# The first twelve weight units of a two-block transformer kernel: one low half on GpSimd, two filler matmuls gone, requests and norm rows in another order

## The reference, cut to what matters

```
mem_n = rmsnorm(mem, mem_norm)
mem_kv = mem_n @ w_mem_kv[i]                  # mk, mv: keys and values of the memory
h = rmsnorm(x, norm_mix[i])
proj = h @ a_w_in[i]
u, b_gate, c_gate, q_mem = jnp.split(proj, ...)
y_tok = _short_conv(u, b_gate, c_gate, a_conv_w[i])
y_mem = _mem_attention(q_mem, mk, mv)
x = x + jnp.concatenate([y_tok, y_mem], axis=-1) @ w_out
```

## Time and profile before

| | |
|---|---|
| median of 3 runs | 930.21 us (928.26 to 930.96) |
| profiled execution, its own time | 925.97 us |
| its span, first to last instruction | 924.2 us |
| PE busy | 913.8 us (99%) |
| DVE busy | 680.7 us (74%) |
| ACT busy | 550.9 us (60%) |
| POOL busy | 76.6 us (8%) |
| transfers, mean | 171 GB/s |

### The profile page before, as it was taken

How to read it: one execution, slowest core, us unless ns; L and a number is a source line. 1 busy time by engine, 2 the same in 40 slices (tenths; PEclk the granted TensorE clock), 3 DMA queues, 4 the chain that set the end, 5 groups by cost and what they waited for, 6 DMA issues and landing times.

```text
span 924.2 us, 16723 instructions
## 1 busy us (share of the span) xinstructions
PE 913.8 (99%) x6111; PEld 810.2 (88%) x6111; DVE 680.7 (74%) x1252; ACT 550.9 (60%) x977; POOL 76.6 (8%) x104
## 2 busy tenths in 40 slices
PE   9999999999999999999999999999999999999997
PEld 8999888888888987888888888999899889999985
DVE  4978678767667788588776686999576767678875
ACT  5654465545455678566554545866577645467783
POOL 0000010111110000100000000000000005532200
PEclk9999999999999999999999999999999999999999
DMA  8665557665655332676655554343245555423312
GB/s 314 221 206 178 190 177 237 223 211 199 219 199 182 114 116 85 207 279 204 206 184 201 184 178 162 139 142 133 69 137 206 179 185 189 142 96 111 116 37 87
DMA packets 43757, 158.11 MB, mean 171 GB/s; under 512 B 5456, under 2 KB 6240, under 8 KB 42928
## 3 DMA queue, kind: packets, MB, share of 16 engines
q1 hardware_dynamic: 41520, 147.79, 47.1%
q0 software_dynamic: 1888, 8.77, 2.7%
q10 hardware_dynamic: 288, 0.72, 0.3%
HBM read 155.82 MB, written 1.05 MB: 170 GB/s over the span
## 4 chain that ended last, share of the span: by engine, by line
PE 91%; DVE 4%; ACT 3%; DMA 1%; issue 1%; SPq 0%; DVEq 0%; ACTq 0%
PE ps L773 16%; PE ps L558 8%; PE ps L559 8%; PE ps L560 8%; PE ps L771 8%; PE ps L613 8%; PE ps L615 8%; PE ps L617 8%; PE ps L768 2%; PE ps L1148 2%; DMA raw<-stream_dram 1%; PE ps L1097 1%; PE ps L1123 1%; PE ps L769 1%; DVE wl L1795 1%; PE ps L596 1%
## 5 line engine op out<-in xcount | busy, mean ns | idle before, releaser
L1795 DVE TENSOR_TENSOR wl<-raw,wh 128x1024 fp32r<-128x1024 f32 x270 | 332.7, 1238 | 100.6 <-ACT wh L1402 50.3
L1234 ACT ACTIVATE wh<-raw 128x1024 fp32r<-128x1024 f32 x174 | 182.1, 1058 | 100.8 <-DMA raw<-stream_dram 89.7
L773 PE MATMUL ps<-hxa,wh 128*128 128x512 f32 x616 | 219.5, 396 | 0.0
L558 PE MATMUL ps<-hxa,wh 128*128 128x256 f32 x672 | 196.4, 292 | 1.1 <-DVE wl L1795 0.5
L559 PE MATMUL ps<-hxa,wh 128*128 128x256 f32 x672 | 189.9, 283 | 0.0
L560 PE MATMUL ps<-hxa,wl 128*128 128x256 f32 x672 | 189.8, 282 | 0.0
L771 PE MATMUL ps<-hxa,wl 128*128 128x256 f32 x616 | 171.9, 279 | 0.0
L1402 ACT ACTIVATE wh<-raw 128x1024 fp32r<-128x1024 f32 x96 | 101.6, 1058 | 59.0 <-PE ps L617 20.7
L773 PEld LDWEIGHTS ps<-hxa,wh 128*128 128x128 f32 x616 | 115.6, 188 | 23.9
L558 PEld LDWEIGHTS ps<-hxa,wh 128*128 128x128 f32 x672 | 128.3, 191 | 8.1 <-issue 5.2
L559 PEld LDWEIGHTS ps<-hxa,wh 128*128 128x128 f32 x672 | 128.5, 191 | 0.2
(11 more groups left out here) (372 smaller groups left out, 1306.5 us busy)
## 6 DMA issues: line engine op xcount, KB each, us to landing
raw<-stream_dram SPq DMA_DIRECT2D x271, 512.0 KB, 3.7
biasm<-bias_dram POOLq DMA_DIRECT2D x12, 192.0 KB, 4.1
w<-w_dram POOLq DMA_DIRECT2D x1, 2048.0 KB, 8.9
mlw<-mlw_dram POOLq DMA_DIRECT2D x1, 1056.0 KB, 6.6
x<-x_dram SPq DMA_DIRECT2D x1, 1024.0 KB, 7.9
mem<-memT_dram SPq DMA_DIRECT2D x1, 1024.0 KB, 8.5
memx<-mem_dram SPq DMA_DIRECT2D x1, 1024.0 KB, 5.8
grow<-rows_dram POOLq DMA_DIRECT2D x2, 512.0 KB, 3.8
```

The source lines that it names most:

```text
L558: pe.matmul(o, wh[:, w_s, w_cols], act[hi], start=start, stop=False, skip_group_check=True)
L773: return pe.matmul(o, wh[:, s % RING, wc], hx[:, k, :, :], start=False, stop=(k == KC - 1), skip_group_check=True)
L1234: act.activation(wh[:, v % RING, :], raw[:, v % RAW, :], ACT.Copy).then_inc(wh_ready, 1)
L1795: dve.tensor_tensor(wl[:, s % RING, :], raw[:, s % RAW, :], wh[:, s % RING, :].bitcast(F32), ALU.subtract).then_inc(wl_ready, 1)
```

## The change

Seven edits, all in the first units:

1. POOL makes the low part of the second half of unit 0, and DVE no longer does. DVE makes all eight low pieces of `hxa` without a break, and then waits for POOL's piece before it goes on with unit 1.
2. The two fillers between the halves of unit 0 are gone.
3. SP requests unit 3 and unit 4 ahead of ident and x, where x stood ahead of unit 4.
4. x comes in two transfers with a semaphore each, and ACT squares the first 128 tokens when they are there.
5. PE makes the residual's norm row after unit 4, where it stood between the halves of unit 4.
6. PE makes the memory's norm row between the two halves of V (units 10 and 11), where it stood between units 9 and 10.
7. DVE copies that row and takes both K units at step 8, ahead of the low part of unit 12, where it did so at step 9, behind it.

```diff
@@ -373,7 +373,8 @@
 
         landed = [sem(f"landed{i}") for i in range(RAW)]
         xT_landed = [sem(f"xT_landed{i}") for i in range(2)]
-        x_landed, grow1_landed, grow2_landed = sem("x_landed"), sem("grow1_landed"), sem("grow2_landed")
+        x_landed = [sem(f"x_landed{t}") for t in range(2)]
+        grow1_landed, grow2_landed = sem("grow1_landed"), sem("grow2_landed")
         mem_landed, cols_landed, ident_landed, consts_landed, bias_landed, bd_landed, mlw_landed, w1_landed = (
             sem(n) for n in ("mem_landed", "cols_landed", "ident_landed", "consts_landed", "bias_landed", "bd_landed",
                              "mlw_landed", "w1_landed"))
@@ -500,10 +501,12 @@
                 sp.wait_ge(wl_ready, u - RAW + 1)
                 sp.dma_start(raw[:, s % RAW, :], stream[u]).then_inc(landed[s % RAW], 16)
 
+            sp.wait_ge(half_lo, 1)
             load(RAW, RAW)
+            load(RAW + 1, RAW + 1)
             sp.dma_start(ident[:], ident_d).then_inc(ident_landed, 16)
-            sp.dma_start(x[:], x_d).then_inc(x_landed, 16)
-            load(RAW + 1, RAW + 1)
+            for t in range(2):
+                sp.dma_start(x[:, t, :], x_d[:, t, :]).then_inc(x_landed[t], 16)
             load(RAW + 2, RAW + 2)
             sp.dma_start(mem[:], memT).then_inc(mem_landed, 16)
             for u in range(RING, RING + RAW):
@@ -828,27 +831,21 @@
                 pe.matmul(ps[:, 2, 0:P], ones[:], ones[:], start=True, stop=True)
             for j, e in enumerate(A_PRE):
                 if e[0] == "V":
-                    project_tokens(PA[e], hxm)
+                    project_tokens(PA[e], hxm, lambda: rrow(ROW_MEM, 2))
                 elif e[0] == "K":
                     project(PA[e], hxm, 8 if e == ("K", 0, 0) else None)
                 elif j < 2:
                     pe.wait_ge(half_lo, j + 1)
                     project_part(PA[e].u, PA[e].bank, hxa, 0, KC // 2, 0 if j == 0 else None)
-                    if j == 0:
-                        for _ in range(2):
-                            pe.matmul(ps[:, 2, 0:P], ones[:], ones[:], start=True, stop=True)
                     weights(PA[e].u)
                     project_part(PA[e].u, PA[e].bank, hxa, KC // 2, KC, 0 if j == 0 else None).then_inc(unit_done, 1)
                 elif e == A_FIRST[-1]:
                     pe.wait_ge(proj_taken, PA[e].free)
                     weights(PA[e].u)
-                    project_part(PA[e].u, PA[e].bank, hxa, 0, KC // 2)
+                    project_part(PA[e].u, PA[e].bank, hxa, 0, KC).then_inc(unit_done, 1)
                     rrow(ROW_A, 0)
-                    project_part(PA[e].u, PA[e].bank, hxa, KC // 2, KC).then_inc(unit_done, 1)
                 else:
                     project(PA[e], hxa)
-                if e == ("K", 0, 1):
-                    rrow(ROW_MEM, 2)
             attend(*PAIRS_A, PA, A_FILL, hxa, PA_OUT, 0, Y_A_SLOTS)
             ffn(PF0, 0, 0, Y_FFN0, 2, ROW_F0)
             pe.wait_ge(consts_landed, 16 * 5)
@@ -1474,8 +1471,8 @@
             split_half(1, 1)
             for u in range(2, 5):
                 split(u)
-            act.wait_ge(x_landed, 16)
             for t in range(2):
+                act.wait_ge(x_landed[t], 16)
                 square(Q_A, t, ajunk)
             root2(Q_A, 0)
             act.wait_ge(cols_landed, 16)
@@ -2023,9 +2020,8 @@
                     .then_inc(wl_ready if half else half_lo, 1)
 
             low_half(0, 0)
-            lows(x0T, hxa, "mix0", 0, 0, 2)
-            low_half(0, 1)
-            lows(x0T, hxa, "mix0", 0, 2, KC)
+            lows(x0T, hxa, "mix0", 0)
+            dve.wait_ge(wl_ready, 1)
             low_half(1, 0)
             low_half(1, 1)
             for u in range(2, 5):
@@ -2069,10 +2065,10 @@
                     dve.reciprocal(mrt, mstd).then_inc(mrt_ready, 1)
                     dve.wait_ge(mrt_ready, 1)
                     diagonal(mrt)
-                if e == ("K", 0, 1):
+                if e == ("K", 0, 0):
                     rows(ROW_MEM, 2, Rm)
-                    take_a(("K", 0, 0))
                     take_a(e)
+                    take_a(("K", 0, 1))
                 if j:
                     ahead_of(PA[e], e)
                 if e in (("u", 1), ("K", 0, 0)):
@@ -2095,7 +2091,8 @@
                 link(dve.tensor_copy(gwh[:], gatew[:]))
                 dve.tensor_tensor(gwl[:], gatew[:], gwh[:].bitcast(F32), ALU.subtract).then_inc(gw_ready, 1)
 
-            dve.wait_ge(x_landed, 16)
+            for t in range(2):
+                dve.wait_ge(x_landed[t], 16)
             ffn(PF0, 0, Q_FFN0, Y_FFN0, 0, PA_OUT["out", 7], "ffn0", 2, ROW_F0, gate_weights)
             residual(1, PF0["out", FC - 1])
             lows_turned(hxb, "kv", 3, TURNED_B)
@@ -2647,6 +2644,9 @@
 
         @block.gpsimd
         def _(pool):
+            pool.wait_ge(wh_ready, 1)
+            nc.gpsimd.tensor_tensor(wl[:, 0, 512:1024], raw[:, 0, 512:1024], wh[:, 0, 512:1024].bitcast(F32),
+                                    ALU.subtract).then_inc(wl_ready, 1)
             pool.wait_ge(unit_done, PF0["gu", 0, 0])
             for dst, src in ((causal[:], causal_d), (rope[:], rope_d), (sel_raw[:], sel_d),
                              (w2[:], w2_d), (gatew[:], gatew_d)):
```

## The result

The changed kernel takes 930.63 us (median of 22 runs, 928.74 to 932.08), the kernel before in the same comparison 928.13 us (median of 22 runs, two of them at 2834 and 5080 us, the other 20 from 925.78 to 931.32). The ratio is 1.0026, 95% interval 1.0017 to 1.0036. The time lies in the predicted range, the sign does not: I forecast 1.1 us less, and it is 2.4 us more by the ratio (2.5 by the medians). The profiled execution took 928.8 us of span against 924.2.

A forecast was written before the change was run, and what follows sets the result against it. PE was taken as the bound, busy 857.07 of 864.2 us from 60 us on. Terms 0.0 (first five units), 0.0 (DVE's start) and 1.06 (memory's row) gave 1.1 us off 930.21: 929.1 us, range 926.6 to 931.3.

The forecast's parts named there:

- Units 0 and 1: First units: POOL's piece runs before DVE's six remaining pieces; PE starts unit 1 near 12.5 instead of 11.94, costing 0.55 us.
- ports: Unit 0: POOL and DVE get in each other's way; a unit 1 start before 12 would show ports were not the limit.
- Unit 4, x, first row: Units 4 and 5: waits of 0.51 and 0.34 us go; unit 5 starts at 24.5 instead of 25.1, 0.65 us gained.
- They have the same bytes to move before `mem` is complete ... term 0: Memory transfer: `mem` lands at 22.5 to 23.5, DVE's gapless stretch unmoved; 0, bounds -0.9 to +1.0 us.
- after 25.8, my zero was wrong: Test at unit 6: its low part starting before 24.8 or after 25.8 would refute the zero for DVE's start.
- The memory's row: Units 9 to 12: row inside V, no wait for row, scores or unit 12; gain 1.06 us.
- Raw slot 0 is freed 1.2 us later, for unit 15, which PE wants after 55: Behind unit 12: later slot for unit 15; low parts of units 13 to 15 at most 0.1 us later.
- DVE's stretch starts earlier: Rival at unit 6's low part: DVE starts sooner; at its bound the gain is 2.1, 928.1 us; chance 0.16.
- Nothing is left: Rival at scores or unit 12: they wait after all, DVE 0.4 us later than reckoned; 930.2 us; chance 0.05.
- POOL is pushed back and the requests slip: Rival in unit 0: POOL waits behind all low pieces, DVE's stretch 1 to 1.5 us late; 930.7 us; chance 0.12.
- Late first operation: Rival: a first operation later than any row shows; chance 0.03.
- The clock: Rival in unit 0: granted clock falls as PE idles from about 8.8 to 9.7 without fillers; chance 0.02.

The follow-up runs named there:

- e11: Kernel before plus POOL's low piece alone, with PE's 64 matmuls on POOL's blocks moved into the middle of the next q unit: 927.38 us, ratio 0.9992.
- e5: e4 with unit 4 requested ahead of x: 929.67 us, ratio 1.0018 to the kernel before.
- e13: e10 with unit 4 requested ahead of x: 928.08 us, ratio 1.0001 to the kernel before.
- e2: Changed kernel with DVE's copy of the memory's row and takes of K behind unit 12's low part again: 929.96 us, ratio 1.0033 to before.
- e10: e4 with PE's 64 matmuls on POOL's blocks moved into the middle of the next q unit: 926.64 us, ratio 0.9983 to the kernel before.
- e6: e4 with the memory row's copy and takes of K ahead of unit 12's low part: 930.58 us, ratio 1.0031 to the kernel before.
- e14: e10 with the takes of K(0,0) and K(0,1) ahead of unit 12's low part: 928.90 us, ratio 1.0013 to the kernel before.
- e4: Changed kernel with the request order, the takes of K and POOL's piece all undone: 928.72 us, ratio 1.0015 to the kernel before.
- e16: Kernel before with only PE's 64 matmuls on POOL's blocks moved, e8 again: 926.70 us, ratio 0.9988 to the kernel before.
- e8: Kernel before with PE's 64 matmuls on POOL's blocks moved into the middle of the following q unit: 927.04 us, ratio 0.9995.
- e1: Changed kernel with x requested ahead of unit 4 again, still in two transfers: 929.82 us, ratio 1.0023 to the kernel before.
- e3: Changed kernel with both the request order and the takes of K undone, POOL's piece kept: 929.82 us, ratio 1.0018 to the kernel before.
- e7: e6 with K(1,0) taken ahead of unit 16's low part: 929.12 us, ratio 1.0019 to the kernel before.
- e9: Changed kernel with PE's 64 matmuls on POOL's blocks moved into the middle of the next q unit: 929.55 us, ratio 1.0013 to before.
- e12: Changed kernel with `mem` requested ahead of unit 5, K(1,0) taken ahead of unit 16's low part, and the 64 matmuls moved: 929.83 us, ratio 1.0017.

## Why the prediction was wrong, point by point

- **Units 0 and 1: right in the end, wrong in who comes first.** POOL's piece was forecast at 8.14 to 9.35 and ran from 8.04 to 9.32 (1.28 us, forecast 1.2; by elements from the 1.01 of the earlier trace rows it would be 1.35), unit 1 at 12.5 (12.23). DVE's six pieces didn't begin at 9.35 but at 8.39; they took 3.19 instead of 2.46 us, a loss of 0.73: the first of them took 1.21 us instead of the 0.47 of the others, until 0.28 us after POOL's end. e11 shows the end of it: nothing at unit 9. That the two take turns, one whole operation after the other, was my estimate; the 12.5 rests on it, and no run shows it. The runs show that DVE's operation beside POOL's took 0.74 us longer and ended 0.28 us behind POOL's end, sooner than one of them takes alone (0.47); two engines that slow each other down would fit as well. The "ports" of the forecast's last line no run shows either: unit 1 at 12.23 was later than the 11.94 of before, and that is all it tells. POOL's row in the changed kernel:

```profile
8.04 1.28 POOL L2648 TENSOR_TENSOR wl<-raw,wh 128x512 fp32r<-128x512 f32 x1 [7.51 <-ACT wh L1453]
```

- **Unit 4, x, first row: right.** No waits, unit 5 at 24.56 (forecast 24.5).
- **"They have the same bytes to move before `mem` is complete ... term 0": this is the step that failed.** I had seen the hole ("the transfers rest for perhaps 1.5 us") and not charged it. The bytes are the same, but the queue's rest (0.53 MB, 1.4 us at 391 GB/s) makes them late unless it would have stood idle later anyway, and until 24 us it did not (the changed kernel's DMA share in 15 to 24 us is 1.00, below). `mem` was forecast at 22.5 to 23.5 and came at 24.5; the low part of unit 6 was 1.65 us late, outside the bounds I gave (0.9). My own test said it: "after 25.8, my zero was wrong". e5 and e13 have the hole without POOL's piece and without the takes: unit 9 at 38.66 and 38.22. What the runs showed in its place: a hole of 0.53 MB in the queue, `mem` 2.0 us and DVE's start 1.65 us later, unit 9 later by 1.64 in this pair of profiles and by some 0.9 on average. The row of the changed kernel's busy time by stretch:

```profile
15.00:24.00 9.00, 9.00 (x78) 9.00 (x77) 3.73 (x7) 4.61 (x7) 0.00 (x0) 1.00 1.00 373
```

- **The memory's row: right, 0.97 of 1.06 us,** no gap at the scores. It was not luck, but it was the smaller half of what the same edit does (next point). e2, e5, e10 and e13 show that the row's move alone gives none of it (9 to 12 in 11.12 to 11.14): it becomes a wait for `mk` of 0.9 to 1.1 us. All of the gain is that of the takes.
- **"Raw slot 0 is freed 1.2 us later, for unit 15, which PE wants after 55": this step failed too.** The 1.2 was right (1.06 against e2), "after 55" also; but I stopped at PE's own unit. I followed neither the transfer (now bunched with the next) nor the take of K(1,0) that stands in DVE's order behind that unit. It costs 1.8 to 2.0 us and outweighs the gain, with the requests untouched as well (e6, e14).
- **The rivals.** "DVE's stretch starts earlier": no, 26.95. "Nothing is left": neither the scores nor unit 12 waited. "POOL is pushed back and the requests slip" had the right price mechanism (`mem` after 24.3 decides; it came at 24.53) and the wrong cause: SP's order, not POOL. Late first operation: no; the piece started at 8.04, behind 7.51 us of waiting for ACT. The clock stayed at 1.00 in unit 0, with a wait of PE of 0.80 us there (1.00 in 0 to 10 us and in 10 to 60). But my argument against its fall was wrong in part: of the 7.1 us of idle time after 60 us, 6.0 lie behind PE's last matmul, where the clock of before is 0.68, and only 1.1 in short waits:

```profile
60.00:918.20 858.20, 857.07 (x5663) 755.05 (x5662) 636.40 (x1170) 512.27 (x913) 76.42 (x100) 1.00 0.49 166
918.20:924.20 6.00, 0.00 (x0) 0.00 (x0) 2.10 (x4) 1.63 (x4) 0.00 (x0) 0.68 0.24 88
```

- **The sum.** Forecast 0 and -1.06; the profiles show +1.64, -0.97, +2.03 = +2.70 up to the second scores, the comparison +2.4. That the time fell into the stated range is luck: two terms were wrong, and the range was centred on a base of 930.21, where before measured 928.13 this time. Around that base it would have missed. What stays open is the wait near 800 us. With the 64 matmuls moved in both, the excess is 1.0013 against 0.9988 to 0.9995 (e16 and e8, other comparisons): 1.7 to 2.3 us, so most of it is made in the first 65 us. Whether the change also makes the wait more frequent was not settled. Something speaks for it: of the 14 profiles of kernels with the change's PE rows 13 had POOL's long chain (over 25 us), of the four without them one (e11). In e4 ten of 12 runs stand at the levels with the wait. And the move of the 64 matmuls brought e4's kernel from 1.0015 to 0.9983 (e10), but before's only to 0.9988 or 0.9995. But these ratios are from different comparisons, and no run here changes the rows of PE alone.

The best versions by their ratios are e10 (0.9983, 0.9972 to 0.9994) and e16 (0.9988, 0.9979 to 0.9997). e16 is before with the 64 matmuls moved; e10 has besides x in two transfers, no fillers and both rows moved. Both lie below before and below the changed kernel; they were not measured in one comparison, so which is faster is open, and e8, the same kernel as e16, was at 0.9995. If anything helped, it was a move that the change didn't have.

## What to carry to other kernels

When a request is moved ahead of another on a queue's engine, ask what the moved one waits for: what stands behind it inherits that wait, as x did here (requested at 13.66 instead of 9.63, behind SP's wait until 12.8). If the queue is full afterwards (share 1.00 in 15 to 24 us), the bytes that should have moved meanwhile (0.53 MB) are charged to the last one wanted (`mem`, 2.0 us). And follow a later free slot past its next user: to the spacing of the requests (1.47 us instead of 2.59), and to whatever stands behind that unit's work in the engine's order (the take of K(1,0), 2.0 us later).

## What the runs showed that I had not expected

- Behind idle times of PE of 1.8 to 2.7 us the granted clock fell to 0.50 in 7 of 12 cases, and behind none of the shorter ones (up to 1.60 us, e6, unit 4). Near 800 us, behind 1.8 us of waiting, it fell in e1, e3 and e5 and stayed in after, e4, e6 and e7; a fall costs 5.38 - 3.71 = 1.67 us. In the head it fell behind 1.77 (e3, unit 4), 1.87 (e9, unit 15), 2.32 (e7, unit 4) and 2.67 us (e12, unit 5), not behind 2.23 (e14, unit 4).
- POOL's 32 operations of 64x120 took 24.1 to 26.8 us for the same work, single ones from 443 to 1499 ns in the changed kernel. DVE runs subtractions of two tensors beside them: one that ran from 776.18 to 777.62 had DVE's subtraction of 775.86 to 777.30 beside it. That these stretch them was not tested.
- With x requested ahead, unit 4's block was ready for its split between 18.6 and 20.9 us from one profile to the next; requested ahead of x, at 16.3 to 16.7. The early request took scatter away (e13: 11 runs within 1.0 us) and made the mean worse (unit 9 at 38.7 against 37.8).
